# Filling a small DRAM table with long rows instead of repeated 8-byte pairs: the expert list of a two-layer diffusion step with MoE

## The chip, the cores and the metric

The kernel runs on one core of a Trainium2 chip, everything in float32, written by hand for each engine: TensorE (PE), VectorE (DVE), ScalarE (ACT), GpSimd (POOL) and the queue of SyncE (SP), with semaphores between them. The metric is the device time of one launch in microseconds (us), lower is better. All transfers, whichever engine issues them, share the core's 16 DMA engines.

## The reference

One inference step of a two-layer backbone over 512 latent and 128 context tokens, width 1024. Each layer has a mixing half (convolution, neighbourhood attention, latent attention, Fourier mixing) and a grouped mixture of experts. What matters here is the second half:

```python
def moe_ffn(h, w_router, b_router, w1, w3, w2):
    s = jax.nn.sigmoid((h @ w_router).astype(jnp.float32))
    sb = s + b_router.astype(jnp.float32)
    grp = sb.reshape(sb.shape[:-1] + (N_EXPERT_GROUPS, EXPERTS_PER_GROUP))
    gsel = jnp.argmax(lax.top_k(grp, TOP_K)[0].sum(-1), axis=-1)
    in_group = (jnp.arange(N_EXPERTS) // EXPERTS_PER_GROUP) == gsel[..., None]
    _, idx = lax.top_k(jnp.where(in_group, sb, NEG_INF), TOP_K)
    ...
    hid = jax.nn.silu(jnp.einsum('bnd,edf->bnef', h, w1)) * jnp.einsum('bnd,edf->bnef', h, w3)
    return jnp.einsum('bnef,efd->bnd', hid * gates[..., None], w2).astype(h.dtype)

# each layer, for both groups of tokens
xs = xs + g1 * mix
xs = xs + g2 * moe_ffn(modulate(xs, norm2[l], sh2, sc2), w_router, b_router, w1[l], w3[l], w2[l])
```

There are 16 experts, and each of the 640 tokens goes to two of them.

## The kernel before

**Stages of a layer.** The body of every engine is a loop over the two layers. A layer first computes the modulation vector (`modulation`, L844: eight 1 MB chunks of `w_ada`, PE L848; VectorE adds the bias at L1349), normalises and transposes the tokens (DVE L1354, PE L865), projects them (PE L839, L881, L882), runs the mixers, and then the experts. SP streams all weights through six ring slots of 1 MB (L568), in the order of the list `CHUNKS`; a slot is loaded again when the stage that read it is through. Behind the eight `w_ada` chunks, SP issues the 2 MB Fourier table (L571) and five more 1 MB chunks (`w_t`).

**The expert list.** `list_d` (L362) is a DRAM table of 640 x 16 entries of two int32 (80 KB): for every expert, which token stands in each place and in which row of `y_d` its result goes. Before each use every entry must hold a filler: token number `N_TOK` (a row of zeros) and a waste row, `2 * N_TOK + b`, b alternating from entry to entry. The real entries are scattered over it by indirect transfers (L759), and POOL reads the list back by rounds (L772).

`empty_lists()` (L622 to L627) writes the filler, with one transfer on POOL's queue. Its source is `none_i`, a tile of 2 x 2 int32 in each partition, with a step of zero over 40 repeats. It is called three times: once in the set-up (L628), ahead of the zeroing of the bias table (L629), and at the end of each layer's expert rounds (L815). The transfers raise `list_zeroed`; POOL waits for it ahead of the layers (L632), ahead of the scatter (L756), and at the very end (L820).

**What stands around the three calls.**

- Start: SP issues 11 small constants (L536, L537), the five tiles of x, 512 KB each (L539), the 8 KB of `c_raw` (L540), and then the `w_ada` chunks. ScalarE and VectorE wait for x and `c_raw` (`x_in`, L1128) and compute `cond` from them (L1129 to L1334), for which PE waits.
- End of a layer: POOL scatters the last expert's rows into `y_d` (L798) and calls `empty_lists()`. When that last scatter has landed, ACT issues ten loads of 512 KB, two for each tile of 128 tokens (L1306, L1307), and after all ten issues works tile by tile: scale on ACT (L1312), then three VectorE operations (L1648, L1650, L1651). The last raises `x_done`. In the first layer, SP's stream of the next layer's weights runs beside this; in the second, nothing is left to stream. Then SP loads `norm_f` (L605), VectorE multiplies (L1658), and ACT stores the output (L1320).

**The tile that the change uses.** `ckv_n` (L302), 5 x 128 floats per partition in the big `arena`, holds the latent keys: VectorE writes it at L1411 and L1415, PE transposes it at L912, POOL stores a part of it at L708. From then until the next layer's L1411 it is idle.

Of the kernel before, what the change touches and what calls it, by code (L numbers as in the profile page):

```python
# [8 lines left out]
I32 = mybir.dt.int32  # L9
# [4 lines left out]
P = 128  # L14
# [5 lines left out]
N_TOK = N_LAT + N_CTX  # L20
# [3 lines left out]
TT = N_TOK // P  # L24
# [6 lines left out]
NE = 16  # L31
# [162 lines left out]
def mixer_kernel(nc, A, O):  # L194
    plan = psum_plan()
    ctx = ExitStack()
    with ctx:
# [3 lines left out]
        def cut(n):  # L201
            top[0] += n
            return top[0] - n
# [4 lines left out]
        def view(at, *shape, parts=P, p0=0):  # L208
            n = int(np.prod(shape))
            v = arena[p0:p0 + parts, at:at + n]  # L210
            if len(shape) == 2:
                return v.rearrange("p (a b) -> p a b", a=shape[0])
            if len(shape) == 3:
                return v.rearrange("p (a b c) -> p a b c", a=shape[0], b=shape[1])
            return v

        def ints(name, *shape):
            return ctx.enter_context(nc.sbuf_tensor(name, [P, *shape], I32))
# [80 lines left out]
        w_fn = view(at_v, 2, 256)  # L299
        wf = view(at_v + 512, 2, 2, 256)  # L300
        v_m = view(at_v, 6, 256)
        ckv_n = view(cut(TT * P), TT, P)  # L302
        kr = view(cut(TT * ROPE), TT, ROPE)
        mods2 = view(at_a + HEADS * 768, 2, 512)
        at_up = cut(768)
# [44 lines left out]
        idx_i = ints("idx_i", 2)  # L350
        out_i = ints("out_i", 2)
        tok_i = ints("tok_i", 2, TT, 2)
        none_i = ints("none_i", 2, 2)

        ps = ctx.enter_context(nc.psum_tensor("ps", [P, 8 * BANK], F32))

# [10 lines left out]
        def sem(name):  # L367
            return ctx.enter_context(nc.semaphore(name))

        def per_layer(name, n):  # L370
            return Signal(sem(name), n)
# [22 lines left out]
        setup_done = sem("setup_done")  # L394
# [31 lines left out]
        routed = per_layer("routed", 1)  # L426
        scattered = per_layer("scattered", 16 * 2 * TT)
        list_zeroed = sem("list_zeroed")
        yg_in = [per_layer(f"yg_in{t}", 32) for t in range(TT)]
        y_first = per_layer("y_first", TT)  # L430
        x_done = per_layer("x_done", TT)
# [29 lines left out]
        def wait(eng, sem, value):  # L461


            eng.wait_ge(sem, value)
            if eng is nc.gpsimd or eng is nc.sync:
                eng.sem_inc(passed, 1)
# [143 lines left out]
        @block.gpsimd  # L610
        def _(pool):
            pool.memset(w_r, 0.0).then_inc(setup_done, 1)
            pool.memset(none_i[:, :, 0], N_TOK).then_inc(setup_done, 1)
            for b in range(2):
                pool.memset(none_i[:, b, 1:2], 2 * N_TOK + b).then_inc(setup_done, 1)
            pool.memset(minus_half, -0.5)
            pool.memset(zeros, 0.0).then_inc(setup_done, 1)
            pool.wait_ge(setup_done, 5)
            pool.dma_start(w_r[:, :, 0:NE], A["w_router"].rearrange("(k p) e -> p k e", p=P)).then_inc(router_in, 16)
            pool.dma_start(h_d[N_TOK:N_TOK + 1, :], zeros[0:1, :]).then_inc(list_zeroed, 16)  # L620

            def empty_lists():  # L622


                pool.dma_start(list_d.rearrange("(p n e) a -> p n e a", p=P, e=2),
                               none_i[:, :, :].unsqueeze(1).broadcast_to((P, N_TOK * NE // P // 2, 2, 2)))\
                    .then_inc(list_zeroed, 16)  # L627
            empty_lists()  # L628
            pool.dma_start(tab.rearrange("h r c k -> (h r) (c k)"), zeros[0:32, 0:TAB_W * GRID_H])\  # L629
                .then_inc(table_zero, 16)  # L630
            pool.wait_ge(table_zero, 16)
# [12 lines left out]
            with pool.Fori(0, DEPTH) as l:  # L644
# [167 lines left out]
                            scatter(e, e % 2)  # L812
                        pool.reg_add(done, done, NE)
                rounds()
                empty_lists()  # L815

            for t in range(TT):
                pool.wait_ge(squares.sem, squares.at(DEPTH, t + 1))
# [505 lines left out]
        def _(dve):  # L1324
# [14 lines left out]
            with dve.Fori(0, DEPTH) as l:  # L1339
# [65 lines left out]
                    dve.tensor_copy(k_n[:, p, 640:768], out[:, N_LAT:N_TOK]).then_inc(bank_of(("pT", 8 + p)), 1)  # L1405

                dve.wait_ge(small_in.sem, small_in.at(l, small_in.per_layer))
                for t in range(TT):
                    out = filled(dve, l, ("pN", t))
                    dve.tensor_copy(v_n[:, t, :], out[:, 0:256])  # L1410
                    dve.tensor_copy(ckv_n[:, t, :], out[:, 256:384]).then_inc(ckv_raw.sem, 1)  # L1411
                    dve.tensor_copy(kr[:, t, :], out[:, 384:416]).then_inc(bank_of(("pN", t)), 1)
# [355 lines left out]
```

## Time and profile before

| what | value |
|---|---|
| runs | 1527.91, 1536.45, 1536.96 us |
| median | 1536.45 us |
| span of the profiled execution, first to last instruction | 1518.1 us |
| the profiled execution's own time | not listed apart from the runs; they are 9.8, 18.4 and 18.9 us above the span |
| mean granted TensorE clock | 0.901 |
| busy: PE / DVE / ACT / POOL | 75% / 30% / 17% / 21% of the span |
| moved by DMA | 260.37 MB, 172 GB/s on average |

Each row of the trace gives when an instruction started and how long it took; what stands in square brackets is the idle time of its engine before it and what ended that. "To landing" is the time from a transfer's issue until its semaphore says that it is complete. The granted clock of TensorE is a share of 2.4 GHz: 1.00 is that level, 0.50 is 1.2 GHz.

### The profile page before, as it was taken

Reading aid. Unit: us, or ns where it says so; the run is one execution under the profiler, and the core shown is the slowest. Engines: PE = TensorE matmul, PEld = TensorE weight load, DVE = VectorE, ACT = ScalarE, POOL = GpSimd, SP = SyncE. Lnnn points to the kernel's source line nnn. Section 1 sums busy time; section 2 is a strip of 40 time slices with the busy share of each in tenths; the row PEclk is TensorE's granted clock in tenths of the full one; section 3 lists DMA queues with packets and bytes.
Section 4 is the critical chain, followed back from the end, with each engine's and each line's share of the span. In section 5 each row is a group of like instructions: output and inputs, shape, how many; then the busy total and the mean of one; then the engine's idle time right before and its main releaser. Section 6 shows DMA issues by size and latency. Waiting matters only on the chain.

```text
span 1518.1 us, 14606 instructions
## 1 busy us (share of the span) xinstructions
PE 1138.9 (75%) x4186; PEld 580.6 (38%) x4186; DVE 450.3 (30%) x987; ACT 253.6 (17%) x564; POOL 311.6 (21%) x430
## 2 busy tenths in 40 slices
PE   0599999579993499998209999948899439998920
PEld 0255545345441244443005554525444214443400
DVE  0211002457134133333052100236632403232316
ACT  0200013145110011111021001223521001111102
POOL 1430011241122311111025001114202231111112
PEclk9699999899996699999559999989999859999965
DMA  8962003364005279988965110336501517878755
GB/s 107 369 216 74 33 1 132 102 251 139 14 28 221 86 289 356 344 327 318 216 262 148 58 56 1 132 73 225 193 1 42 221 42 288 334 298 321 294 66 185
DMA packets 56690, 260.37 MB, mean 172 GB/s; under 512 B 9776, under 2 KB 11200, under 8 KB 40752
## 3 DMA queue, kind: packets, MB, share of 16 engines
q1 hardware_dynamic: 32768, 185.53, 35.6%
q0 software_dynamic: 20256, 60.95, 11.7%
q10 hardware_dynamic: 3600, 13.11, 3.3%
q8 instruction: 30, 0.49, 0.1%
q14 instruction: 36, 0.29, 0.1%
HBM read 233.01 MB, written 28.94 MB: 173 GB/s over the span
## 4 chain that ended last, share of the span: by engine, by line
PE 60%; DMA 22%; DVE 6%; issue 5%; POOL 2%; SPq 2%; ACT 1%; ACTq 1%; POOLq 0%; DVEq 0%
PE ps L1080 10%; PE ps L839 10%; PE ps L1030 9%; DMA arena<-in_w 9%; PE ps L1099 5%; DMA arena<-expert_out 5%; PE ps L882 5%; PE ps L881 4%; DMA arena<-in_w_ada 3%; PE ps L840 3%; DMA arena<-in_norm 2%; PE ps L848 2%; PE ps L1007 2%; PE ps L977 2%; PE ps L900 2%
## 5 line engine op out<-in xcount | busy, mean ns | idle before, releaser
L1080 PE MATMUL ps<-arena 128*128 128x512 f32 x512 | 239.9, 624 | 26.4 <-DMA arena<-in_w 22.8
L839 PE MATMUL ps<-arena 128*128 128x512 f32 x352 | 180.4, 594 | 3.7 <-DVE arena L1372 3.7
L1080 PEld LDWEIGHTS ps<-arena 128*128 128x128 f32 x512 | 100.0, 199 | 162.7 <-issue 157.9
L1030 PE MATMUL ps<-arena 128*128 128x512 f32 x320 | 138.8, 593 | 2.4 <-DVE arena L1498 2.4
L848 PE MATMUL ps<-arena 128*32 128x512 f32 x384 | 60.1, 744 | 82.2 <-DMA arena<-in_w_ada 78.5
L1099 PE MATMUL ps<-arena 128*128 128x512 f32 x256 | 115.4, 594 | 3.1 <-issue 3.1
L1596 DVE COPY arena<-ps 128x512 f32<-128x512 f32 x32 | 22.1, 692 | 308.0 <-PE ps L1069 308.0
L639 POOL TENSOR_SCALAR arena<-arena 128x1 f32<-128x1 f32 x45 | 13.3, 295 | 486.4 <-ACT arena L1171 224.0
L840 PEld LDWEIGHTS ps<-arena 128*128 128x128 f32 x352 | 66.9, 190 | 84.1 <-issue 84.1
L798 POOL DMA_INDIRECT expert_out<-arena,out_i x32 | 31.5, 985 | 301.2 <-DVE arena L1617 265.7
L1030 PEld LDWEIGHTS ps<-arena 128*128 128x128 f32 x320 | 60.2, 190 | 76.8 <-issue 76.8
L882 PE MATMUL ps<-arena 128*128 128x512 f32 x160 | 81.7, 592 | 0.0
L1069 PE MATMUL ps<-arena 128*128 128x128 f32 x256 | 35.0, 282 | 56.9 <-DMA arena<-expert_in,idx_i 56.9
L881 PE MATMUL ps<-arena 128*128 128x416 f32 x160 | 68.9, 512 | 0.0
L728 POOL TENSOR_SCALAR arena<-arena 128x384 f32<-128x384 f32 (+1 forms) x48 | 49.3, 1031 | 92.0 <-DVE arena L1491 92.0
L987 PE MATMUL ps<-arena 128*128 128x128 f32 x272 | 44.2, 279 | 31.6 <-POOL arena L728 29.7
L840 PE MATMUL ps<-arena 128*128 128x128 f32 x352 | 67.7, 274 | 0.0
L1099 PEld LDWEIGHTS ps<-arena 128*128 128x128 f32 x256 | 46.2, 190 | 49.8 <-issue 49.8
L1606 DVE RECIPROCAL arena<-arena 128x256 f32<-128x256 f32 x32 | 56.1, 1754 | 1.1
L839 PEld LDWEIGHTS ps<-arena 128*128 128x128 f32 x352 | 53.6, 192 | 4.2 <-issue 4.1
L848 PEld LDWEIGHTS ps<-arena 128*32 128x32 f32 x384 | 10.6, 122 | 116.3 <-DMA arena<-in_w_ada 94.6
L1007 PE MATMUL ps<-arena 128*64 128x128 f32 (+1 forms) x304 | 35.6, 365 | 25.5 <-ACT arena L1232 25.5
(237 smaller groups left out, 1376.3 us busy)
## 6 DMA issues: line engine op xcount, KB each, us to landing
arena<-in_w SPq DMA_DIRECT2D x96, 1024.0 KB, 9.1
arena<-in_w_ada SPq DMA_DIRECT2D x48, 1024.0 KB, 7.6
arena<-in_w_t SPq DMA_DIRECT2D x10, 1024.0 KB, 30.1
arena<-expert_out ACTq DMA_DIRECT2D x20, 512.0 KB, 28.5
arena<-in_w_out SPq DMA_DIRECT2D x8, 1024.0 KB, 5.9
arena<-mod_rows POOLq DMA_DIRECT2D x16, 512.0 KB, 8.5
arena<-in_w_n SPq DMA_DIRECT2D x8, 928.0 KB, 4.8
expert_in<-arena POOLq DMA_DIRECT2D x10, 512.0 KB, 3.0
```

The costliest lines, as they stand in the source:

```text
L728: pool.tensor_scalar(pr, pr, rowinv[:, u % 4:u % 4 + 1], None, ALU.mult).then_inc(probs_ready.sem, 1)
L839: mm(out[:, 0:N_LAT], lhsT, rhs_of[:, 0:N_LAT], start=(k == 0), stop=(k == n - 1))
L840: return mm(out[:, N_LAT:N_TOK], lhsT, rhs_of[:, N_LAT:N_TOK], start=(k == 0), stop=(k == n - 1))
L848: ins = mm(out[32 * j:32 * j + 32, 0:512], cond[:, k, :], w[:, j, :], start=(k == ks[0]), stop=(k == ks[-1]), skip_group_check=True)
L881: mm(out[:, 0:416], hk, w[k // 2][:, k % 2, 0:416], start=(k == 0), stop=(k == KD - 1))
L882: ins = mm(out[:, 512:1024], hk, w[k // 2][:, k % 2, 416:928], start=(k == 0), stop=(k == KD - 1))
L987: ins = tr(out[:, c * P:(c + 1) * P], probs[:, u % 4, c * P:(c + 1) * P], ident)
L1007: ins = mm(out[lo:lo + 64, 0:width], by_head(v, hh), pt, start=(c == 0), stop=(c == n - 1), skip_group_check=True)
L1030: ins = mm(out[:, n * 512:(n + 1) * 512], yT[:, k, t * P:(t + 1) * P], w[k // 2][:, k % 2, n * 512:(n + 1) * 512], start=(k == 0), stop=(k ...
L1080: ins = mm(out, hsT[b][:, k, :], w[:, k, :], start=(k == 0), stop=(k == KD - 1))
L1099: ins = mm(out[:, n * 512:(n + 1) * 512], hidT[:, f, :], w[:, f, n * 512:(n + 1) * 512], start=(f == 0), stop=(f == 1))
L1606: dve.reciprocal(f, f).then_inc(silu_chain, 1)
```

## The change

`none_i` is no longer a tile of its own: it is the first 640 bytes per partition of `ckv_n`, seen as 160 int32. `empty_lists` now fills these with three memsets on POOL (one of 80 numbers, two of 40), waits for them with a new semaphore, and writes the table with a source that is contiguous in each partition, as the destination is. Since the tile is shared, VectorE waits for `list_zeroed` before it writes `ckv_n`. The set-up's three small memsets of `none_i` go.

```diff
-        ckv_n = view(cut(TT * P), TT, P)
+        at_none = cut(TT * P)
+        ckv_n = view(at_none, TT, P)
...
-        none_i = ints("none_i", 2, 2)
+        none_i = view(at_none, N_TOK * NE // P * 2).bitcast(I32).rearrange("p (n e a) -> p n e a", e=2, a=2)
...
+        none_ready = sem("none_ready")
...
             pool.memset(w_r, 0.0).then_inc(setup_done, 1)
-            pool.memset(none_i[:, :, 0], N_TOK).then_inc(setup_done, 1)
-            for b in range(2):
-                pool.memset(none_i[:, b, 1:2], 2 * N_TOK + b).then_inc(setup_done, 1)
             pool.memset(minus_half, -0.5)
             pool.memset(zeros, 0.0).then_inc(setup_done, 1)
-            pool.wait_ge(setup_done, 5)
+            pool.wait_ge(setup_done, 2)
...
-            def empty_lists():
-
-
-                pool.dma_start(list_d.rearrange("(p n e) a -> p n e a", p=P, e=2),
-                               none_i[:, :, :].unsqueeze(1).broadcast_to((P, N_TOK * NE // P // 2, 2, 2)))\
-                    .then_inc(list_zeroed, 16)
-            empty_lists()
+            def empty_lists(n):
+
+                pool.memset(none_i[:, :, :, 0], N_TOK).then_inc(none_ready, 1)
+                for b in range(2):
+                    pool.memset(none_i[:, :, b, 1], 2 * N_TOK + b).then_inc(none_ready, 1)
+                wait(pool, none_ready, n)
+                pool.dma_start(list_d.rearrange("(p n e) a -> p n e a", p=P, e=2), none_i).then_inc(list_zeroed, 16)
+            empty_lists(3)
...
-                empty_lists()
+                empty_lists(l * 3 + 6)
...
                 dve.wait_ge(small_in.sem, small_in.at(l, small_in.per_layer))
+                dve.wait_ge(list_zeroed, l * 16 + 32)
                 for t in range(TT):
                     out = filled(dve, l, ("pN", t))
                     dve.tensor_copy(v_n[:, t, :], out[:, 0:256])
```

POOL's instructions at the start of the program; `arena` is the big tile in which w_r, zeros and now also the filler lie, and the numbers are rows x elements. Before:

```order
L617 MEMSET arena 128x1024
L619 DMA arena<-in_w_router 128x8x16 [waits setup_done]
L620 DMA expert_in<-arena 16x1x64
L625 DMA expert_list<-none_i 5120x1x4
L629 DMA bias_tab<-arena 32x512
L644 UNCONDITIONAL_BRANCH [waits cond_ready,list_zeroed,table_zero]
```

After:

```order
L616 MEMSET arena 128x1024
L618 DMA arena<-in_w_router 128x8x16 [waits setup_done]
L619 DMA expert_in<-arena 16x1x64
L623 MEMSET arena 128x80
L625 MEMSET arena 128x40 x2
L627 DMA expert_list<-arena 128x160 [waits none_ready]
L629 DMA bias_tab<-arena 32x512
L644 UNCONDITIONAL_BRANCH [waits cond_ready,list_zeroed,table_zero]
```

The transfer of 5120 rows of 4 numbers has become one of 128 rows of 160, and the memsets now stand between it and the transfer ahead of it. The same happens at the end of the expert rounds.

VectorE, ahead of the first write into `ckv_n` (the second row of the loop that starts at L1410 in the kernel before, L1411 in the changed one). Before:

```order
L1405 COPY arena<-ps 128x128
L1407 ISA
L464 REGISTER_ALU [waits small_in]
L1410 COPY arena<-ps 128x256 [waits psum_full]
L1411 COPY arena<-ps 128x128
```

After:

```order
L1405 COPY arena<-ps 128x128
L1407 ISA
L1408 ISA [waits small_in]
L466 REGISTER_ALU [waits list_zeroed]
L1411 COPY arena<-ps 128x256 [waits psum_full]
L1412 COPY arena<-ps 128x128
```

One wait has been added; nothing else has moved on VectorE.

## Rows read from the trace of the kernel before

**Rows 1.** The page's chain that ended last, shares of the span.

```profile
PE 60%; DMA 22%; DVE 6%; issue 5%; POOL 2%; SPq 2%; ACT 1%; ACTq 1%; POOLq 0%; DVEq 0%
```

**Rows 2.** The same chain in order of time: start us, us, what; three DMA pieces.

```profile
11.39 31.20 DMA arena<-in_w_ada
...
746.29 39.97 DMA arena<-expert_out
...
1459.13 29.74 DMA arena<-expert_out
```

**Rows 3.** Line 625: issue ns min/median/max, first and last start; time to landing.

```profile
L625 POOL DMA_DIRECT2D expert_list<-none_i x3: 1981/1992/2011, 4.3 to 1454.5; - x3
...
DMA to landing us min/median/max: 26.3/29.8/30.3
```

**Rows 4.** Stretches: us, busy by engine, granted clock, DMA share, GB/s.

```profile
12.00:34.00 22.00, 0.00 (x0) 0.00 (x0) 0.00 (x0) 0.00 (x0) 0.00 (x0) 1.00 0.93 82
726.00:744.00 18.00, 1.93 (x8) 0.20 (x8) 0.00 (x0) 0.00 (x0) 0.60 (x2) 0.60 0.98 57
1457.00:1484.00 27.00, 0.00 (x0) 0.00 (x0) 0.00 (x0) 0.00 (x0) 0.00 (x0) 0.50 0.78 64
...
758.00:765.00 7.00, 0.00 (x0) 0.00 (x0) 2.23 (x2) 1.15 (x1) 0.00 (x0) 0.50 1.02 414
...
165.00:245.00 80.00, 80.00 (x223) 40.25 (x223) 8.44 (x30) 9.18 (x30) 11.89 (x27) 1.00 0.22 75
```

**Rows 5.** DMA issues over the whole run: KB each, median us to landing.

```profile
arena<-in_c_ident SPq DMA_DIRECT2D x1, 64.0 KB, 1.8
...
arena<-in_w_router POOLq DMA_DIRECT2D x1, 64.0 KB, 3.7
...
out_y<-arena ACTq DMA_DIRECT2D x5, 512.0 KB, 3.0
...
arena<-in_norm_f SPq DMA_DIRECT2D x1, 512.0 KB, 3.3
```

**Rows 6.** Timeline of the start: issues of x and c, ScalarE's and VectorE's first steps.

```profile
6.16 2.79 SPq L539 DMA_DIRECT2D arena<-in_x_all  x5
8.99 1.37 SPq L540 DMA_DIRECT2D arena<-in_c_cols  x1
...
37.77 0.22 ACT L1129 ACTIVATE arena<-arena 128x16 f32<-128x16 f32 x1 [35.50 <-DMA arena<-in_c_cols]
...
66.88 0.69 DVE L1349 TENSOR_TENSOR arena<-ps,arena 128x512 f32<-128x512 f32 x1 [27.85 <-PE ps L848]
```

**Rows 7.** Timeline of the first layer's end.

```profile
717.33 0.97 POOL L798 DMA_INDIRECT expert_out<-arena,out_i  x1 [3.50 <-DVE arena L1617]
...
729.94 0.35 ACTq L1306 DMA_DIRECT2D arena<-expert_out  x1
...
786.29 1.15 ACT L1312 ACTIVATE arena<-arena 128x1024 f32<-128x1024 f32 x1 [2.35 <-DMA arena<-expert_out]
```

**Rows 8.** Timeline of the second layer's end.

```profile
1456.87 0.34 ACTq L1306 DMA_DIRECT2D arena<-expert_out  x1
1457.23 0.97 ACTq L1307 DMA_DIRECT2D arena<-expert_out  x1
...
1459.13 6.60 ACTq L1307 DMA_DIRECT2D arena<-expert_out  x1
...
1470.07 1.50 ACTq L1307 DMA_DIRECT2D arena<-expert_out  x1
1484.43 1.15 ACT L1312 ACTIVATE arena<-arena 128x1024 f32<-128x1024 f32 x1 [31.96 <-DMA arena<-expert_out]
...
1493.88 1.28 DVE L1648 SCALAR_TENSOR_TENSOR arena<-arena 128x1024 f32<-128x1024 f32 x1
...
1497.60 1.28 DVE L1648 SCALAR_TENSOR_TENSOR arena<-arena 128x1024 f32<-128x1024 f32 x1
...
1503.89 1.22 DVE L1651 TENSOR_TENSOR arena<-arena 128x1024 f32<-128x1024 f32 x1
```

## The prediction

> **What bounds the kernel now.** I began with the chain that ended last. PE holds 60% of it and DMA 22% [rows 1]. 22% of 1518 us is 334 us; most of that is the stream of expert weights, which the change leaves alone. The chain in order of time shows what the page's shares hide: three single pieces of 31.20, 39.97 and 29.74 us in which nothing but a transfer is waited for [rows 2]. They lie at the start, at the end of layer 0 and at the end of layer 1.
>
> The second view was line 625, the list's filler. It is issued three times, and the first and last issues, at 4.3 and 1454.5 us, stand just ahead of the first and the last piece. Each transfer of 80 KB needs 26.3 to 30.3 us to land [rows 3], though a plain 64 KB load (in_c_ident) lands in 1.8 us and 512 KB in 3.0 to 3.3 us [rows 5].
>
> The third view was the stretches [rows 4]. In each of the three places the DMA engines are 78 to 98% busy and move only 57 to 82 GB/s. Between 758 and 765 us, with the same queues working, they move 414 GB/s. So the engines are occupied by something that carries few bytes, and it lasts as long as the filler's transfer. No engine computes in two of the three stretches. That is my reading: 5120 pieces of 16 bytes take turns with x, with the weights and with the expert results, on all 16 engines, and every other transfer waits for its turn.
>
> **The change part by part.**
>
> *The transfer.* The order of the instructions shows 5120 rows of 4 numbers becoming 128 rows of 160. That is the shape of an ordinary load, and I price it by its nearest row: in_c_ident, also 128 rows, 64 KB, 1.8 us; at 80 KB about 2 us [rows 5]. Its issue on POOL took 2.0 us [rows 3]; it will be shorter, and nobody waits for it.
>
> The Trainium skill, "DMA: Bandwidth & Descriptors" (section "Anatomy of one DMA"), fits a GpSimd transfer as 2.0 us plus bytes over 436 GB/s; for 80 KB that is an estimated 2.2 us, before and after alike, and the change would be worth nothing. This trace disagrees, with 26.3 us at the least [rows 3].
>
> *Start.* Before, ScalarE's first step waits until 37.77 us for c_cols, which is queued behind the five tiles of x [rows 6]. With free engines the first tile, issued at 6.16 us, should land 3.3 us later (the 512 KB load of norm_f, [rows 5]), and each of the other four 512 KB / 414 GB/s = 1.27 us after the one before: 6.16 + 3.3 + 5.1 = 14.5 us. c_cols is 8 KB, behind them; I give it 1 us: 15.5 us. Everything behind it in this stage (cond, the w_ada chunks in their queue, POOL's small loads, VectorE's L1349 at 66.88 us) hangs on this landing or on the same queue and should move along rigidly. Gain: 37.8 - 15.5 = 22.3 us. Lower bound: only what is lost in the measured stretch, 22 x (1 - 82/414) = 17.6 us [rows 4]. Upper bound: c_cols right behind x, and its own cost nothing, 23.3 us.
>
> *End of layer 0.* Here SP's weight stream runs beside the ten loads of expert results, and the engines are full anyway. So I count bytes: from 726 to 744 us they run at 57 GB/s instead of 414, which loses 18 x (1 - 57/414) = 15.5 us [rows 4]. The last tile's L1312, at 786.29 us [rows 7], comes that much earlier. Upper bound: the last scatter, issued at 717.33 us, now lets ACT start at 729.94 us [rows 7]; a part of these 12.6 us lies in the slow stretch (726 to 729.9, 3.9 us). If it all comes on top, 19.4 us. It is counted once, since the bytes that the loads fetch are the same. Lower bound: 11 us, where weights and results don't pack as well once they start together (a quarter and more of the 15.5 lost; a choice, no row shows it).
>
> *End of layer 1.* No weights run here. The ten loads are issued from 1456.87 us on, and L1312 of the first tile starts at 1484.43 us [rows 8]. It needs two things: the first two loads, and that ACT is through with its ten issues. The loads: the second is issued at 1457.23 us and lands 3.3 + 1.3 us later, 1461.8 us. The issues: the ten took from 1456.87 to 1471.57 us, 6.60 of it one stalled issue [rows 8]; without the excess of that one (it would take some 0.8 us, as the issues around it did) they end at 1465.8 us, and at the unstalled 0.7 to 0.8 us each at 1464.4 us. I take 1464.4. Gain: 20.0 us. Behind it VectorE is the limit at 3.72 us a tile (1493.88 to 1497.60, [rows 8]), so after: 1464.4 + 1.3 + 5 x 3.72 = 1484.3 us for x_done, where it is 1505.1 us now (1503.89 + 1.22). Gain: 20.8 us. What is late next here is VectorE's chain and no longer a transfer. Upper bound: issues at 0.34 us each, so that the loads' landing decides: 2.6 us more, 23.4. Lower bound: the stall of 6.6 us has another cause and stays, 1484.43 - 1471.6 = 12.9, and the 0.8 of the tiles: 13.7 us.
>
> *What is added.* Three memsets of at most 80 numbers per row stand ahead of each filler transfer, and a wait for them. On POOL they delay the transfer and, behind it, the zeroing of the bias table, the loads of the next layer's small parameters (layer 0's end), and nothing at the last end. All that is behind them has over 20 us of slack there, since it is needed only when x is ready; cost nothing. If that cover were gone it would be the memsets' own time, under 1 us each call. VectorE's new wait for list_zeroed, with the copies of v and ckv and the whole layer's attention behind it, stands in the projection stage: the transfer that it needs was issued over 150 us earlier in both layers. Cost nothing.
>
> **Sum.** 22.3 + 15.5 + 20.8 = 58.6 us. The span goes from 1518.1 to 1459.5 us. The runs before are 9.8 to 18.9 us above that span; I subtract from their median: 1536.45 - 58.6 = 1477.9, say 1478 us. By the bounds: 17.6 + 11 + 13.7 = 42.3 us at the least (1494), 23.3 + 19.4 + 23.4 = 66.1 at the most (1470). With the 9 us by which the runs before differ, the forecast's own range is 1464 to 1497.
>
> **The rivals.**
>
> *A. A piece costs little, and the filler is only part of the stall.* For: w_router is a load of 1024 pieces of 64 bytes, and it lands in 3.7 us, 1.9 us later than in_c_ident with 128 pieces [rows 5]: 2.1 ns for each piece more. At that price 5120 pieces take 10.6 us and not 28, the rest would be someone else's, and the gain is 3 x (10.6 - 2) = 26 us: 1511 us. Against: reads from DRAM may be cheaper than writes into it, and three landings within 4 us of each other in three different surroundings speak for the transfer's own cost [rows 3]. The Trainium skill, same page (section "Bandwidth", measured), has a floor of some 10.5 ns a packet, by which 320 packets per engine would be an estimated 3.4 us and the collapse wholly someone else's; the gain by this, three times some 3 us, would leave about 1527 us.
>
> *B. The start has a second cause.* SP issues 11 small constants there, some in rows of 64 bytes or less, and x stands behind them. If these hold x up as long as the filler does, the start gives nothing and the rest stays: 15.5 + 20.8 = 36.3 us, 1500 us. Against: 12 to 34 us moves 82 GB/s, long after those were issued, and looks like the other two stretches [rows 4].
>
> *C. The new transfer is as slow, or the collapse isn't its doing at all.* No change, 1536 us. The order of instructions speaks against the first, the coincidence of all three places against the second.
>
> *D. Slower, by the clock.* In the idle stretches the granted clock is 0.50 or 0.60, and in the projection stage (165 to 245 us) it is 1.00 [rows 4]. If some 60 us less rest made the chip hold TensorE at 1.2 GHz in a later stage of dense work, each us of that work would cost one more: from 59 us of such work on the gain is gone, and with the whole stage of 165 to 245 us it would be 80 - 58.6 = 21 us slower, 1558 us. Against: the clock is low during and behind idle time, not during dense work, so less idling can hardly lower it.
>
> *E. More than my upper bound,* for instance where weights that arrive earlier cut other waits: 1465 us.
>
> **How the numbers follow.** Forecast 0.76, A 0.08, B 0.06, C 0.03, D 0.02, E 0.05. The range is the forecast's own, 1464 to 1497: A, C, D and most of B lie outside, about 0.19. Faster by over 1% (about what a measurement of this kernel tells from no change): forecast, A at 1511, B and E, 0.95; within 1%: C, 0.03; slower: D, 0.02.
>
> **What would show it.** The filler's landing falls from 26 to 30 us to 2 to 4 us. ScalarE's first step starts at 15 to 17 us; VectorE's L1349 at about 44.6. The stretch behind layer 0's last scatter moves over 350 GB/s throughout. In layer 1 ACT's ten issues take 7 to 9 us, and its first scaling starts 10 us or less after the first issue. The three DMA pieces in the chain shrink, and the projection stages between are unchanged in length. Wrong would be: a landing under 4 us with any of the stretches still under 100 GB/s (then the cause was not the filler), or a stage of dense matmuls that got longer (D).

## The result, and the profile after

| | before | after |
|---|---|---|
| runs | 1527.91, 1536.45, 1536.96 us | 1449.48, 1456.22, 1461.47 us |
| median | 1536.45 us | 1456.22 us |
| span of the profile | 1518.1 us | 1447.9 us |

The ratio is 0.9515 (95% interval 0.947 to 0.956): 80.2 us less by the medians and 70.2 us less by the spans, where 58.6 us were forecast. 1456 us lies below the range of 1464 to 1497. Here and below the medians are of all runs, while a ratio and its interval are formed from the fast runs alone, so that it need not be the quotient of the medians. The listed spans of the changed kernel's runs are 1.6 us under their times. By that the profile of the kernel before belongs to an execution of some 1520 us (an estimate), 17 us under its median. This turned out to be a part of the answer.

The chain by engine, from the page of the changed kernel, and its transfer pieces in order of time (start, us, what), which answer to [rows 1] and [rows 2]:

```profile
PE 63%; DMA 18%; DVE 7%; issue 6%; POOL 2%; SPq 2%; ACT 1%; ACTq 0%; DVEq 0%; POOLq 0%
```

```profile
10.21 9.84 DMA arena<-in_w_ada
...
706.87 36.27 DMA arena<-expert_out
...
1409.52 5.10 DMA arena<-expert_out
```

The first piece has fallen from 31.2 to 9.8 us and the last from 29.7 to 5.1. The middle one is hardly shorter (40.0 to 36.3), though that stage gained 16 us. It now starts earlier in its stage, and SP's weight stream takes its share of the bandwidth as before. A piece of the chain measures what was waited for, not what a change can take out of it.

The filler's line in the changed kernel (issue min/median/max; time to landing), answering to [rows 3]:

```profile
L627 POOL DMA_DIRECT2D expert_list<-arena x3: 585/592/594, 5.2 to 1407.7; - x3
...
DMA to landing us min/median/max: 1.9/2.4/8.5
```

Stretches of the changed kernel (us, busy of PE, PEld, DVE, ACT, POOL, granted clock, DMA share, GB/s), answering to [rows 4]:

```profile
12.00:34.00 22.00, 7.47 (x40) 0.97 (x40) 0.90 (x4) 5.85 (x11) 14.54 (x26) 0.79 1.03 354
...
703.00:721.00 18.00, 5.80 (x24) 0.60 (x24) 0.00 (x0) 0.00 (x0) 1.07 (x2) 0.52 1.02 358
...
1410.00:1422.00 12.00, 0.00 (x0) 0.00 (x0) 5.96 (x5) 4.45 (x5) 0.90 (x1) 0.50 0.94 344
```

The DMA engines are as busy as before or busier, but carry 344 to 358 GB/s instead of 57 to 82. The two stretches at layer 1's end, split by queue (packets, MB, share of the 16 engines' time; q10 is ACT's queue with the expert results, q0 is POOL's with the filler). Before, 1457 to 1484 us:

```profile
q10 hardware_dynamic: 443, 1.63, 69.0%
q0 software_dynamic: 96, 0.08, 8.7%
```

After, 1410 to 1422 us:

```profile
q10 hardware_dynamic: 1125, 4.13, 94.4%
```

A packet of the expert results holds 3.7 KB in both, and takes 0.69 x 16 x 27 us / 443 = 0.67 us of an engine's time beside the filler and 0.944 x 16 x 12 us / 1125 = 0.16 us without it. The filler's own queue holds the engines for only 8.7% of their time. At the start it is the same: from 12 to 34 us SP's queue, with x and the weights, takes 89.1% and POOL's 3.7%.

The start, answering to [rows 6]:

```profile
15.20 0.22 ACT L1129 ACTIVATE arena<-arena 128x16 f32<-128x16 f32 x1 [12.92 <-DMA arena<-in_c_cols]
...
45.81 0.69 DVE L1349 TENSOR_TENSOR arena<-ps,arena 128x512 f32<-128x512 f32 x1 [29.36 <-PE ps L848]
```

And the end of the second layer, answering to [rows 8]:

```profile
1409.15 0.34 ACTq L1306 DMA_DIRECT2D arena<-expert_out  x1
1409.52 0.45 ACTq L1307 DMA_DIRECT2D arena<-expert_out  x1
...
1413.93 0.47 ACTq L1307 DMA_DIRECT2D arena<-expert_out  x1
1414.64 1.15 ACT L1312 ACTIVATE arena<-arena 128x1024 f32<-128x1024 f32 x1 [9.88 <-DMA arena<-expert_out]
```

**A table by stage.** To see where the time went I cut every run's chain at the same events: the first transposition of the normalised tokens in each layer (PE L865), and the start of the last expert's down projection (PE L1099). These are the cuts in the kernel before:

```profile
70.93 5.68 PE ps L865 x36
...
712.04 3.69 PE ps L1099 x8
...
797.66 5.83 PE ps L865 x36
...
1448.17 3.69 PE ps L1099 x8
```

and in the changed one:

```profile
49.87 5.73 PE ps L865 x26
...
688.57 3.69 PE ps L1099 x8
...
758.18 3.69 PE ps L865 x16
...
1400.45 3.69 PE ps L1099 x8
```

So the kernel before spends 70.9 us at the start, 797.66 - 712.04 = 85.6 us at layer 0's end and 1518.1 - 1448.17 = 69.9 us at layer 1's end. The changed one spends 49.9, 69.6 and 47.5 us. The three places give 21.0 + 16.0 + 22.4 = 59.4 us (59.6 before rounding, which is the figure in the expectations below). The other 10.8 us of the spans' difference come from in between, where the change does nothing. The table below holds all runs, their chains cut in this way; "between" is the span less the three rounded numbers. In e6 and e9 single transfers stand ahead of everything, so only the two ends can be compared.

| run | start | layer 0's end | layer 1's end | between | median of the runs |
|---|---|---|---|---|---|
| before | 70.9 | 85.6 | 69.9 | 1291.7 | 1536.5 |
| before, second profile (e5) | 74.4 | 91.2 | 76.2 | 1283.0 | 1529.2 |
| changed | 49.9 | 69.6 | 47.5 | 1280.9 | 1456.2 |
| changed again (e1) | 49.9 | 69.7 | 47.5 | 1286.8 | 1461.7 |
| changed, five rounds (e10) | 49.8 | 69.8 | 47.8 | 1282.3 | 1453.5 |
| old filler in the set-up only (e2) | 77.5 | 69.3 | 47.3 | 1278.0 | 1474.9 |
| old filler at the ends only (e3) | 50.1 | 91.3 | 73.7 | 1272.3 | 1496.5 |
| old filler in a quiet place (e4) | 50.0 | 69.7 | 47.8 | 1278.6 | 1459.2 |
| new filler in a quiet place (e7) | 50.8 | 69.5 | 47.7 | 1298.6 | 1459.0 |
| 32-byte pieces everywhere (e8) | 50.4 | 70.8 | 48.4 | 1280.4 | 1455.8 |
| the same, five rounds (e11) | 50.5 | 69.7 | 48.2 | 1297.0 | 1451.2 |
| before, with single transfers ahead (e6) | - | 91.3 | 74.5 | - | - |
| before, with single transfers ahead (e9) | - | 90.5 | 72.8 | - | - |

Wherever the old filler is absent from a stage, the stage repeats within 1.5 us from profile to profile. The part in between differs by 26 us, though the kernels do the same work there (but for the filler itself, which e4 and e7 have there). With the old filler at the ends, the two ends together take 163.3 to 167.4 us in four profiles (e3, e5, e6, e9), taken on three chips; the first profile of the kernel before, with 155.5 us, is the odd one.

### The profile page after: what moved, and what is told of

It reads as the page before. It is cut to its first block, busy times and chain, and to the rows that moved or that the text cites. A ratio compares the mean times of both kernels' runs of the same rounds, so it can differ in the third digit from the quotient of the medians.

```text
span 1447.9 us, 14619 instructions
## 1 busy us (share of the span) xinstructions
PE 1139.9 (79%) x4186; PEld 581.8 (40%) x4186; DVE 450.0 (31%) x987; ACT 253.9 (18%) x564; POOL 310.5 (21%) x436
## 4 chain that ended last, share of the span: by engine, by line
PE 63%; DMA 18%; DVE 7%; issue 6%; POOL 2%; SPq 2%; ACT 1%; ACTq 0%; DVEq 0%; POOLq 0%
PE ps L839 10%; PE ps L1080 10%; PE ps L1030 10%; DMA arena<-in_w 9%; PE ps L1099 5%; PE ps L882 5%; PE ps L881 4%; DMA arena<-expert_out 3%; PE ps L840 3%; PE ps L848 2%; PE ps L1007 2%; DMA arena<-in_w_ada 2%; PE ps L977 2%; PE ps L900 2%; DMA arena<-in_norm 2%
## 5 line engine op out<-in xcount | busy, mean ns | idle before, releaser
L1080 PE MATMUL ps<-arena 128*128 128x512 f32 x512 | 234.1, 611 | 23.4 <-DMA arena<-in_w 19.9
L1080 PEld LDWEIGHTS ps<-arena 128*128 128x128 f32 x512 | 97.7, 195 | 156.5 <-issue 151.8
L1099 PE MATMUL ps<-arena 128*128 128x512 f32 x256 | 115.4, 594 | 3.1 <-issue 3.1
L840 PEld LDWEIGHTS ps<-arena 128*128 128x128 f32 x352 | 66.9, 190 | 84.2 <-issue 84.2
L1030 PEld LDWEIGHTS ps<-arena 128*128 128x128 f32 x320 | 60.2, 190 | 76.9 <-issue 76.9
L882 PE MATMUL ps<-arena 128*128 128x512 f32 x160 | 81.7, 592 | 0.0
L1099 PEld LDWEIGHTS ps<-arena 128*128 128x128 f32 x256 | 46.1, 190 | 49.8 <-issue 49.8
L839 PEld LDWEIGHTS ps<-arena 128*128 128x128 f32 x352 | 53.6, 192 | 3.8 <-issue 3.6
L1069 PEld LDWEIGHTS ps<-arena 128*128 128x128 f32 x256 | 30.4, 146 | 58.8 <-issue 58.8
```

Of the source, the lines that this page charges most:

```text
L839: mm(out[:, 0:N_LAT], lhsT, rhs_of[:, 0:N_LAT], start=(k == 0), stop=(k == n - 1))
L840: return mm(out[:, N_LAT:N_TOK], lhsT, rhs_of[:, N_LAT:N_TOK], start=(k == 0), stop=(k == n - 1))
L882: ins = mm(out[:, 512:1024], hk, w[k // 2][:, k % 2, 416:928], start=(k == 0), stop=(k == KD - 1))
L1030: ins = mm(out[:, n * 512:(n + 1) * 512], yT[:, k, t * P:(t + 1) * P], w[k // 2][:, k % 2, n * 512:(n + 1) * 512], start=(k == 0), stop=(k ...
L1069: ins = tr(ps[:, k * P:(k + 1) * P], hs[:, b, k * P:(k + 1) * P], ident)
L1080: ins = mm(out, hsT[b][:, k, :], w[:, k, :], start=(k == 0), stop=(k == KD - 1))
```

## The experiments

**e1, the changed kernel again.** No edit.

> The changed kernel once more, beside the kernel before on the same chip. Between the two profiles on record the three places of the filler give 21.1 + 16.0 + 22.5 = 59.6 us, and 10.6 us more come from stages in between (a wait for the norm2 load in the first layer's attention, passes over expert weights at a lower granted clock in the second layer). Theory N (these 10.6 us and the 10 us by which the medians differ more than the spans are run-to-run spread of both kernels): the medians differ by 55 to 70 us this time, and the stages in between come out different again, with either sign. Theory S (they are an effect of the change): the medians differ by 75 to 85 us again and the same stages are shorter.

Measured: 1461.65 us against 1531.46 us of the kernel before on the same chip, 69.8 us less; ratio 0.957 (0.950 to 0.964). The three stages are the same to 0.1 us, and "between" is 5.9 us longer. One place shows why: the wait for the norm2 row in the first layer's attention, first in the changed kernel, then in this run of the same kernel:

```profile
254.54 10.03 DMA arena<-in_norm
```

```profile
254.17 17.32 DMA arena<-in_norm
```

Theory N holds for the stages in between: they came out different again, so their 10.8 us are spread, not gain. Over the eleven profiles other than e6's and e9's the 22 such waits lie between 8.7 and 18.2 us, with or without the old filler. It does not hold for the other half of what it says: the medians differ by 69.8 us again and not by 59.6, and by e5 the larger part of that gap is the stalls themselves and not spread.

**e2 and e3, one place at a time.** The changed kernel, with the old transfer back in the set-up (e2) or at both layers' ends (e3), from a tile of its own with 16 bytes per partition, filled in the set-up:

```diff
+            def empty_lists_old():
+                pool.dma_start(list_d.rearrange("(p n e) a -> p n e a", p=P, e=2),
+                               none4[:, :, :].unsqueeze(1).broadcast_to((P, N_TOK * NE // P // 2, 2, 2)))\
+                    .then_inc(list_zeroed, 16)
-            empty_lists(3)
+            empty_lists_old()
```

That is e2, where the count that the later calls wait for is lowered to match; in e3 the call at the layer's end is the one replaced.

> The changed kernel, with the old filler of 5120 pieces in the set-up alone. Theory P (each old filler costs its own place while it shares the DMA engines, and nothing else): slower than the changed kernel by 21 us, ScalarE's first step at 37 to 38 us, both layer ends as in the changed kernel. Rival B (the start had a second cause, here with the new filler gone from it as well): less than 10 us. Rival S (places act on each other, so that undoing one costs more than its share): over 28 us.

> The changed kernel, with the old filler at the end of both layers and the new one in the set-up. Theory P: slower than the changed kernel by 16 + 22.5 = 38.5 us, of which 22.5 behind the second layer's last scatter; ScalarE's first step at 15.2 us as in the changed kernel. Together with the run of the old filler in the set-up this adds up to 59.6 us. Rival S (places act on each other): the two together differ from 59.6 us by over 10 us.

Measured: e2 1474.91 us (ratio to before 0.967, 0.958 to 0.975), e3 1496.51 us (0.979, 0.972 to 0.987). Each old filler spoils its own stage and no other: 27.6 us at the start in e2, 21.7 and 26.2 us at the ends in e3. That is theory P, but with larger numbers than the first profile gave (21.0, 16.0, 22.4), 75.5 us together. ScalarE's first step in e2, and the filler's landing in e2 and e3:

```profile
43.40 0.22 ACT L1137 ACTIVATE arena<-arena 128x16 f32<-128x16 f32 x1 [41.12 <-DMA arena<-in_c_cols]
```

```profile
expert_list<-none POOLq DMA_DIRECT2D x1, 80.0 KB, 34.2
```

```profile
expert_list<-none POOLq DMA_DIRECT2D x2, 80.0 KB, 33.4
```

37 to 38 us had been expected, 43.4 came: the old filler itself took 34 us to land and not 30. By the medians the two costs add up to only 13.3 + 34.9 = 48 us over e1. That is 11 us under 59.6, which was the mark set for rival S (places act on each other), and 27 us under the 75.5 us of the stages. The stages speak against S: the two runs' places add up to what the kernel before shows in e5, and no other place moves. What is missing lies in "between", which is short in both profiles (1278.0 and 1272.3 us). With medians of four runs that spread over 12 to 13 us each I take it for spread and the stages for the better witness; that it is spread is not shown.

**e4, the old filler where nobody waits.** The kernel before, its 5120 pieces unchanged, but issued once per layer in the projection stage:

```diff
                 ins.then_inc(bias_ready.sem, 1)
+                empty_lists()
...
-                empty_lists()
```

The call in the set-up goes too, and POOL's waits for `list_zeroed` count one transfer less.

> The kernel before, its transfer of 5120 pieces unchanged, but issued once per layer in the projection stage (behind the bias table's adds, some 110 us into the layer), and neither in the set-up nor at a layer's end. Theory P (the pieces cost nothing where no other transfer is waited for): as fast as the changed kernel within 5 us, or 2 us faster, with the filler still taking 20 to 30 us to land. Rival Q (the old filler costs POOL or the DMA rings something wherever it stands, or the loads of nk and nv behind it delay attention): slower than the changed kernel by 15 us or more.

Measured: 1459.2 us, ratio to before 0.955 (0.947 to 0.962), 2.5 us under e1. The filler and its neighbours on POOL's queue:

```profile
arena<-in_nk_t POOLq DMA_DIRECT2D x2, 128.0 KB, 15.5
arena<-in_nv_t POOLq DMA_DIRECT2D x2, 128.0 KB, 17.6
...
expert_list<-none_i POOLq DMA_DIRECT2D x2, 80.0 KB, 22.9
```

The pieces are as slow as they were, 22.9 us, and the loads of nk and nv behind them take 15.5 and 17.6 us, where they took 2.7 and 2.6 us in the kernel before. The whole gain is there all the same: neither wait has become a cost ("between" is 1278.6 us, one of the shorter ones). So what cost 60 to 75 us was not the transfer's own time but what it did to the transfers beside it in the three places.

**e5, the kernel before a second time.** No edit.

> The kernel before, profiled a second time. In the runs with the old filler back in one place it took 33 to 34 us to land and cost 27.6 us at the start, 21.6 and 26.2 us at the two ends (75.4 us together), where the first profile of the kernel before showed 26 to 30 us and 59.4 us. Theory V (that first profile was of a favourable execution, and the filler's price differs from one execution to the next): this profile shows landings of 28 to 35 us and 60 to 76 us for the three places against the changed kernel. Rival W (the price is fixed for each program, and depends on where the filler's source lies): 26 to 30 us to land and 59 to 60 us again.

Measured: 1529.2 us, beside 1526.9 us of the same kernel in the eleven runs of the same session (ratio 1.005, 1.0004 to 1.009). Two sets of runs of one program thus differ by 2.3 us, and by slightly more than the interval allows. Line 625, the stretch of the start, and the chain's pieces:

```profile
DMA to landing us min/median/max: 32.0/32.6/35.6
```

```profile
12.00:34.00 22.00, 0.00 (x0) 0.00 (x0) 0.00 (x0) 0.00 (x0) 0.00 (x0) 1.00 0.96 65
```

```profile
10.79 35.02 DMA arena<-in_w_ada
...
732.36 45.49 DMA arena<-expert_out
...
1459.49 35.69 DMA arena<-expert_out
```

The same program shows landings of 32 to 36 us where the first profile had 26 to 30, and every piece is longer. Its three stages stand 24.5 + 21.6 + 28.7 = 74.8 us over the changed kernel's. Rival W is out, since the program is the same. Theory V holds: the price of the filler is not fixed by the program, and the profile that the forecast was made from had a cheap one. The ends of e6 and e9 say the same: against the changed kernel's 117.1 us, the two ends cost 48.7 and 46.2 us there, 47.9 in e3 and 50.3 in e5, but 38.4 in the first profile. Whether the price differs between executions or between chips is open, since the record does not say on which chip the first profile was taken.

**e6 and e9, single transfers with nothing beside them.** The kernel before, with eight (e6) and ten (e9) transfers one at a time ahead of everything; SP waits for them, so the times of these two kernels (1585.52 and 1637.73 us) hold the transfers as well and say nothing more.

```diff
+            for i, (dst, src) in enumerate(probes):
+                pool.dma_start(dst, src).then_inc(probe_done, 16)
+                pool.wait_ge(probe_done, 16 * (i + 1))
```

> The kernel before with eight transfers ahead of all others, one at a time and with nothing beside them: 80 KB from the chip's memory to DRAM in pieces of 16 bytes from a repeated source, of 16 bytes from a source that doesn't repeat (into DRAM rows of 32 bytes), of 64, 160, 320 and 640 bytes, then 5120 pieces of 16 bytes from DRAM into the chip's memory, and 128 rows of 512 bytes to DRAM. Theory C (the number of pieces decides): the two of 16 bytes land in 21 to 25 us each (22.9 us in the quiet place), 64 bytes in 6 to 8, 160 bytes in 3.5 to 5, 640 bytes in 2. Rival D (the repeated source is what costs, since all pieces of a row read the same 16 bytes): the second one lands in half the time or less. For the direction: if it matters, reading in pieces of 16 bytes is faster by a factor of 1.5 or more than writing.

Measured (80 KB each, us to landing; a and b 16-byte pieces, c 64, d 160, f 640 bytes; arena<-probe_b 16-byte pieces read from DRAM). Not shown are 320-byte pieces with 2.1 us and the 128 rows of 512 bytes with 1.8 us:

```profile
probe_a<-arena POOLq DMA_DIRECT2D x1, 80.0 KB, 20.8
...
probe_b<-arena POOLq DMA_DIRECT2D x1, 80.0 KB, 15.9
...
probe_c<-arena POOLq DMA_DIRECT2D x1, 80.0 KB, 2.9
...
probe_d<-arena POOLq DMA_DIRECT2D x1, 80.0 KB, 2.3
...
probe_f<-arena POOLq DMA_DIRECT2D x1, 80.0 KB, 1.9
...
arena<-probe_b POOLq DMA_DIRECT2D x1, 80.0 KB, 6.6
```

Theory C expected 6 to 8 us for the 1280 pieces of 64 bytes, 3.5 to 5 for those of 160, and over 21 for b; 2.9, 2.3 and 15.9 us came. Rival D expected half of a for b or less, and got three quarters. And 5120 pieces of 16 bytes read from DRAM land in 6.6 us instead of 15.9. Neither the number of pieces nor the repeated source explains this. A second row of e6, the DMA engines' busy share over 3 to 24 us in 40 slices of 0.53 us:

```profile
DMA  0000098979993040300000000000000000000000
```

Probe a is issued at 3.0 us and lands at 23.8. The engines have done recorded work from about 5.6 to 12 us; then they rest for 12 us while the transfer is still not complete. For the 16-byte pieces read from DRAM (issued at 50.8 us) the recorded work ends at about 55.5 us and the transfer lands at 57.4, 2 us later. So most of probe a's time passes after the engines' recorded work. That the writes pile up behind the engines, on the way into DRAM, is what this suggests; no run shows where they are.

> As the run of the single transfers, ten more, each alone. Before: 16-byte pieces written to DRAM land in 20.8 us (dense, repeated source) and 15.9 us (every 32 bytes, source not repeated), read from DRAM in 6.6 us; the filler in 2560 pieces of 32 bytes lands in 6.4 us. Theory R (what costs is a write into DRAM of less than 32 bytes, whatever the source is): dense from a source that doesn't repeat 20 to 22 us; repeated source into every 32nd or every 64th byte 14 to 18; 16-byte pieces inside the chip's memory and read from DRAM 5 to 8; 2560 pieces of 16 bytes half of the dense one, 9 to 12; 5120 of 8 bytes 18 or more. 32-byte pieces that start on a 32-byte boundary 4 to 7, and, if it is whole units of 32 bytes that count, 12 or more when each starts 16 bytes off one. Rival N (the number of pieces alone, with a limit between 2560 and 5120): 2560 pieces of 16 bytes in under 7 us and 5120 inside the chip's memory in 15 or more. Rival D (repeated source): the dense one from a source that doesn't repeat in under 16 us.

Measured (h 16 bytes dense, source not repeated; i every 32 bytes; j every 64 bytes; k and m 32-byte pieces on a 32-byte boundary; l 32-byte pieces 16 bytes off one; arena<-arena inside the chip's memory; arena<-probe_h read from DRAM; n 8-byte pieces; o 2560 pieces of 16 bytes):

```profile
probe_h<-arena POOLq DMA_DIRECT2D x1, 80.0 KB, 20.9
...
probe_i<-arena POOLq DMA_DIRECT2D x1, 80.0 KB, 16.2
...
probe_j<-arena POOLq DMA_DIRECT2D x1, 80.0 KB, 11.9
...
probe_k<-arena POOLq DMA_DIRECT2D x1, 80.0 KB, 4.2
...
probe_l<-arena POOLq DMA_DIRECT2D x1, 80.0 KB, 8.8
...
probe_m<-arena POOLq DMA_DIRECT2D x1, 80.0 KB, 4.2
...
arena<-arena POOLq DMA_DIRECT2D x1, 80.0 KB, 6.6
...
arena<-probe_h POOLq DMA_DIRECT2D x1, 80.0 KB, 6.3
...
probe_n<-arena POOLq DMA_DIRECT2D x1, 40.0 KB, 25.1
...
probe_o<-arena POOLq DMA_DIRECT2D x1, 40.0 KB, 11.1
```

Theory R holds: what costs is a write into DRAM that does not fill whole units of 32 bytes, be it that the piece is shorter or that it starts off the boundary. The repeated source plays no part (20.9 us for h, 20.8 for a). 2560 pieces of 16 bytes cost half of 5120 (o), so no limit on the number lies between. Two of my numbers were off: pieces 64 bytes apart are cheaper than expected (11.9, not 14 to 18), and 32-byte pieces off their boundary take twice the time of aligned ones but not three times (8.8, not 12 or more).

**e7, both edits.** The changed kernel, its long-row filler moved to the quiet place of e4.

> The changed kernel with its long-row filler issued once per layer in the projection stage, neither in the set-up nor at a layer's end: both edits together. Theory P: the new filler already costs nothing where it stands, so the same as the changed kernel within 1%, with the start 49.9, the first end 69.6 and the second 47.5 us. Rival: the 2 us that the filler takes, and the zeroing of the bias table behind it, still count at an end: 2 to 5 us faster.

Measured: 1459.03 us, ratio to before 0.957 (0.951 to 0.963); the stages are the changed kernel's but for 0.9 us more at the start. Moving the new filler away as well wins nothing, as theory P said.

**e8 and e11, pieces of 32 bytes.** The kernel before with a filler tile twice as wide, its memsets widened with it: 2560 pieces of 32 bytes in the three old places.

```diff
-        none_i = ints("none_i", 2, 2)
+        none_i = ints("none_i", 4, 2)
...
-                pool.dma_start(list_d.rearrange("(p n e) a -> p n e a", p=P, e=2),
-                               none_i[:, :, :].unsqueeze(1).broadcast_to((P, N_TOK * NE // P // 2, 2, 2)))\
+                pool.dma_start(list_d.rearrange("(p n e) a -> p n e a", p=P, e=4),
+                               none_i[:, :, :].unsqueeze(1).broadcast_to((P, N_TOK * NE // P // 4, 4, 2)))\
```

> The kernel before with pieces of 32 bytes, so 2560 and not 5120 of them, in all three places. Theory C (pieces count): the filler lands in 13 to 17 us, and about half of the gain appears: 30 to 38 us faster than the kernel before. Rival (a threshold: any small piece spoils the engines as long as one such transfer is under way, whatever the count): landing over 20 us, gain under 15 us.

Measured: 1455.82 us, 71.1 us less than the kernel before beside it (1526.9), ratio 0.955 (0.948 to 0.963): the whole gain and not half of it. Landings, min/median/max:

```profile
DMA to landing us min/median/max: 6.4/6.6/10.6
```

Both expectations missed: it is neither half nor nothing. It was this run that sent me to the second set of single transfers. 16 more bytes per partition in a tile of its own do nearly what 640 do.

> The changed kernel in five rounds for the size of the gain. From the profiles: 59.4 us against the first profile of the kernel before, 74.8 us against its second; by theory V the mean lies between, so the medians differ by 65 to 75 us (ratio 0.951 to 0.957).

> Pieces of 32 bytes in all three places in five rounds. By its profile its three places stand 0.5, 1.1 and 0.9 us behind the changed kernel's, so it should be slower than that by 2.5 us, which may not show: 0 to 5 us slower. If the 15 us between the kernels' extremes hide something else, up to 10 us slower.

Measured, on one chip with 11 runs of the kernel before at a median of 1525.38 us: the changed kernel 1453.54 us (ratio 0.949, 0.943 to 0.955), 71.8 us less; 32-byte pieces 1451.23 us (0.952, 0.947 to 0.956). The 71.8 us are within the 65 to 75 expected, though the ratio of 0.949 lies just outside the expected 0.951 to 0.957. By the medians the 32-byte pieces are 2.3 us faster and not 0 to 5 us slower as expected, but the intervals overlap: the two can't be told apart by time. The stages of e8 and e11 put the 32-byte pieces 1.4 to 2.6 us behind the first profile of the changed kernel. No version beats the changed kernel clearly.

## Why the prediction was right or wrong

**The cause of the three stalls was right.** The filler's pieces held up the transfers beside them in three places. Each stall goes away with the edit, comes back when the old form is put back in that place (e2, e3), and goes away too when the old form is moved from its neighbours (e4).

**How it does so was read too simply.** The prediction has 5120 pieces taking turns with the other transfers on the 16 engines. By the queues' shares at layer 1's end, the filler's queue takes 8.7% of the engines' time; the rest of their busy time goes to the expert results' own packets, which take 0.67 us each instead of 0.16. And it is not the number of pieces: 2560 pieces of 32 bytes bring the whole gain (e8), while 2560 of 16 bytes still need 11.1 us alone and 5120 read from DRAM only 6.3 (e9). The forecast did not suffer by this, since it priced the stalls by the bytes that were not moved. At layer 0's end that held well: the stage moves 21.46 MB before and after.

**Against the profile it was made from, the sum was right.** Start: ScalarE's first step at 15.20 us, forecast 15.5; the stage 21.0 us shorter, forecast 22.3 (L1349 came at 45.8 us and not 44.6; the chunks behind did not move quite rigidly). Layer 0's end: 16.0 us, forecast 15.5 by counting bytes. Layer 1's end: 22.4 us, forecast 20.8. There ACT's ten issues took 0.34 to 0.74 us each, 5.3 us in all, where 7.5 had been assumed and 7 to 9 named as the sign: 0.7 to 0.8 us was itself a price under the filler. Together 59.4 us, forecast 58.6. Of the other signs one missed: the filler at layer 0's end, beside the weights, lands in 8.5 us and not in 2 to 4; nobody waits for it.

**What failed is the step from that profile to the time.** The forecast took the three stalls as constants of the kernel, and all its bounds stem from the same rows. They are not constants; in e5 every one of them is above its upper bound (24.5, 21.6 and 28.7 us, where the terms were 22.3, 15.5 and 20.8 and the bounds 23.3, 19.4 and 23.4). In e5 the filler of the same program lands in 32.0 to 35.6 us instead of 26.3 to 30.3, and the places cost 74.8 us instead of 59.4. e2 and e3 show 75.5 us as well. The medians differ by 80.2, 69.8 and 71.8 us in three comparisons. So the term that was mis-sized is the stall per place: about 25 us on the whole, 19.5 us in the forecast. A sign of it was there: the span lay 9.8 to 18.9 us under the three runs. I listed this, then subtracted a gain read from a favourable execution from a median of ordinary ones. With 75 us in place of 58.6 the same sum gives about 1461 us. The working of the range is also off: the bounds of 1470 and 1494 us are said to be widened by 9 us, but 1464 and 1497 are only 6 and 3 us away; 9 us each way give 1461 to 1503, and 1456 lies outside of that too. Either way the widening allowed for a shift of the base, not for a stall that grows.

**In between.** The 10.8 us that the spans lost outside of the three places are spread (e1). And 8 to 10 of the 80.2 us by the medians are luck of the first comparison, with three runs on each side: the two later ones give 69.8 and 71.8.

**The rivals.** A (a piece costs little, since w_router's cost little): its price is that of a read, and wrong here. 5120 pieces of 16 bytes land in 6.3 us when they are read, and in 20.9 when they are written. I had noted that writes might be dearer; short writes into DRAM are. Its sum had two slips: 10.6 us is what 4992 more pieces add, so the landing by that price is 12.4 us; and the 3.4 us worked out from the Trainium skill's 10.5 ns a packet ("DMA: Bandwidth & Descriptors", section "Bandwidth") share the pieces out over 16 engines, while the page has that figure from 64 packets of a whole transfer in 0.67 us. Taken so, 5120 pieces would be an estimated 54 us. This case's runs agree with neither: 20.9 us written and 6.3 us read. B (a second cause at the start): no, the old filler alone brings 27.6 us back there (e2), and nothing at the start when it stands at the ends (e3). C: no, the new transfer lands in 1.9 to 8.5 us and the stalls are gone. D (the clock): no; "between" is no longer in the changed kernel, and the mean granted clock is 0.907 to 0.918 in its three profiles where it is 0.901 and 0.905 in those of the kernel before. E foresaw more than my upper bound, by another mechanism than the true one. The two costs put at nothing are nothing. The memsets with their wait: the stages of e7, with the memsets elsewhere, are no shorter. VectorE's new wait: its first write behind it is released by PE's L882 and not by the filler, which had landed 150 us earlier (161 us in the second layer, where the row starts at 865.13 us):

```profile
157.43 0.42 DVE L1411 COPY arena<-ps 128x256 f32<-128x256 f32 x1 [11.57 <-PE ps L882]
```

## What to carry to other kernels

A transfer's price can lie not in its own landing but in what runs beside it. So look for small writes into DRAM near every wait for a transfer; make their pieces 32 bytes or more on 32-byte boundaries, or move them to where nobody waits. The mark in a profile is a stretch with busy DMA engines and a sixth to a quarter of the bandwidth (here 57 to 82 GB/s for 344 to 358). And before a stall is subtracted from a median, take a second profile: the same three places cost 59 us in one and 75 us in the other. That the first profile's span lay 10 to 19 us under the runs was a warning here, but no sure sign: the profile of e2 is of its fastest run and shows a large stall.

## What the runs showed of the hardware

- One filler of 5120 pieces of 16 bytes lands in 20.8 to 20.9 us alone. Per DMA engine that is (20.9 - 1.9) / 320 = 59 ns a piece, if 1.9 us (128 rows of 640 bytes) is the base and the pieces are spread over all 16. A 32-byte write on a boundary costs (4.2 - 1.9) / 160 = 14 ns, a 16-byte read from DRAM (6.3 - 1.9) / 320 = 14 ns, an 8-byte write 72 ns, a 32-byte write off its boundary 43 ns.
- Small writes cost more the closer they lie: 20.9 us dense, 16.2 us every 32 bytes, 11.9 us every 64 bytes. That several small writes meet in one larger unit of DRAM is an explanation that these numbers suggest; no run shows it.
- The Trainium skill, "DMA: Bandwidth & Descriptors" (section "Specifications"), gives 512 bytes as the least transfer for full rate and says that below this a read-modify-write takes place. Full rate was not tried here, and no run shows a read-modify-write. In landing times of 80 KB into DRAM the large step lies at 32 bytes: from 64-byte to 640-byte pieces the landing only goes from 2.9 to 1.9 us.
- The engines can have finished all recorded work 12 us before such a transfer lands (e6). Beside other work they show as 78 to 98% busy at 57 to 82 GB/s, most of it with the other transfers' own packets (69.0% against 8.7% at layer 1's end), each of which takes four times as long. Why reads of other DRAM tensors are held up was not tried.
- With the filler gone, ACT issues a 512 KB load at layer 1's end in 0.34 to 0.74 us; beside it the first takes 0.34 us, the others 0.73 to 1.50, and one 6.60 us.
